# Hybrid attention and SSD block on one core: B and C split into rounded and low parts, their product as three rounded products

## Chip, core and metric

One core of a Trainium2 chip runs the whole kernel. The time is that of the device in microseconds, and lower is better. Four compute engines matter: TensorE (matmuls; its weight loads are listed apart as PEld), VectorE (DVE), ScalarE (ACT) and GpSimd (POOL), with SyncE (SP) issuing most of the DMAs. Each engine runs its own list of instructions in order and waits on semaphores for the others.

## What is computed

One layer of a block with 256 tokens, width 2048 and float32 data. Attention and a bidirectional Mamba-2 SSD stand side by side, then an MLP. The part that the change touches is the SSD: for each of 8 groups, B and C (128 states x 256 tokens, after convolution and SiLU) are multiplied, masked and weighted with decays.

```python
def ssd_chunked(x, dt, A, Bm, Cm):
    xc = (x.astype(jnp.float32) * dt[..., None]).reshape(b, nc, CHUNK, g, h, p)
    Bc = Bm.reshape(b, nc, CHUNK, g, n)
    Cc = Cm.reshape(b, nc, CHUNK, g, n)
    ...
    cb = jnp.einsum('bclgn,bcsgn->bgcls', Cc, Bc)
    y_diag = jnp.einsum('bgcls,bghcls,bcsghp->bclghp', cb, Lmat, xc)
```

The SSD's result y is gated, `y * silu(z)`, and normalised within each group, then multiplied together with the attention's by w_out; the MLP is `x + jnp.square(jax.nn.relu(hm)) @ w_down`, with hm the normalised x times w_up.

## The kernel before

The large products stream the weights. A unit is a block of 512 columns of a weight matrix with all 2048 rows; it comes in 8 chunks of 256 rows, and a chunk is one slot of the program. A chunk is loaded into one of 8 buffers raw (SyncE, which waits until TensorE has used the buffer's last chunk), ScalarE copies it rounded into w_hi (line 495), VectorE subtracts to get w_lo, which lies in raw's place (line 836), and TensorE multiplies it in three rounded products, low x high, high x low, high x high: 12 matmuls of 128x512. ScalarE and VectorE work on the chunk four slots ahead (LEAD = 4). All matmuls go through one helper line, 1256; the rest of an operation's name in the profile tells which it is.

The small work of the SSD and the attention is laid between the slots. A window has 24 slots, and two groups of the SSD are handled in it. For a group, slots are counted as k from its start; the next group starts 12 slots later (GROUP_SLOT). The order is written by hand and is this:
- k = 3 to 9 of the previous group: VectorE's convolution of the new group (conv, line 876); k = 10: ScalarE's tanh (conv_t, line 543); k = 11: VectorE's silu writes xbc, whose parts 0 and 1 are x, part 2 is B, part 3 is C (line 881).
- k = 0: TensorE's group_products, after the slot's chunk: four transposes of x into the PSUM bank M0 (line 1332), then, once M1 is free, the product of B and C into M1, two matmuls of 128x256 in full precision.
- k = 1: VectorE masks the product (mask_cb, lines 887 and 889) and scales x (line 850).
- k = 2 to 5: VectorE multiplies the decays (mix, line 859). ScalarE makes the decays of the next group in slots 6, 7, 8 and 12 (line 533 to 539), and waits there for y_done, the semaphore of the y products that use the same buffers mix.
- k = 5 and 7: TensorE's y products from mix. k = 8: VectorE's gate (lines 895, 900). k = 9: squares (ScalarE line 560, VectorE 964 to 968). k = 10: TensorE sums them over the partitions. k = 11: VectorE's mean_sq (line 905), ScalarE's Ln and Exp (lines 563, 565), each with a table load. k = 12: VectorE's group_norm, four operations that end with gate_t (lines 910 to 918). k = 13 and 14: the result rounded and its low part.

Slot k = 12 of one group is slot k = 0 of the next. In it VectorE does the w_lo of the slot, then group_norm; TensorE does its chunk, then group_products of the new group.

The groups 1 to 6 start in windows of the projection, and group 7 in the first window of attention, between 0 and 400 us of the program; group 0 starts in the first window, at slot 20, where no group is ahead of it.

Of the kernel before, what the change touches and what calls it, by code (L numbers as in the profile page):

```python
# [28 lines left out]
P = 128  # L29
SEQ, D_MODEL = 256, 2048  # L30
# [49 lines left out]
def build(nc, x, norm_mix_g, w_in, q_norm_g, k_norm_g, rel_bias, conv_w, conv_b, dt_bias, a_log,  # L80
# [18 lines left out]
    with ctx:  # L99
# [77 lines left out]
        rnorm = place("rnorm", [P, SEQ], at=at_of(lo2, 1024))  # L177
        newton = place("newton", [P, SEQ], at=at_of(lo2, 1024))

        sq_hi = place("sq_hi", [P, SEQ], f32r, at=cat_base + 32768)  # L180
        sq_lo = place("sq_lo", [P, SEQ], f32r, at=lo2[0] - 3072)
        gate_n = gate_t
# [65 lines left out]
        def sem(name):  # L248
            return ctx.enter_context(nc.semaphore(name))
# [36 lines left out]
        p_transposed, pT_ready, pv_done, att_hi, att_lo = (sem(n) for n in (  # L286
            "p_transposed", "pT_ready", "pv_done", "att_hi", "att_lo"))
        gate_summed = sem("gate_summed")
        first_tile_done, dt_half = sem("first_tile_done"), sem("dt_half")
        xres_in, added, squared_mid, mid_step = sem("xres_in"), sem("added"), sem("squared_mid"), sem("mid_step")  # L290
        rest_copied, hid_added, relu_squared, hid_hi_s, hid_lo_s, down_added, out_stored = (sem(n) for n in (
# [174 lines left out]
        def _(act):  # L466
# [74 lines left out]
            def conv_tanh_of(G):  # L541
                act.wait_ge(conv_step, 20 * (G + 1))
                act.activation(conv_t[:, :, :], conv[:, :, :], ACT.Tanh).then_inc(conv_tanh, 1)

            def next_group(G, i, k):

                if k in DECAY_SLOTS:
                    decays(G, DECAY_SLOTS[k])
                if k == 10:
                    conv_tanh_of(G)  # L550

            def ssd_slot(s, m, more=True):

                for i, o in enumerate(GROUP_SLOT):
                    G, k = 2 * m + i, s - o
                    if not 0 <= k < 16 or (i == 2 and not more):
                        continue
                    if k == 9:
                        act.wait_ge(gated, G + 2)
                        act.activation(gate_sq[:, :, :], gate[:, :, :], ACT.Square).then_inc(gate_squared, 1)  # L560
                    if k == 11:
                        act.wait_ge(m1_free, G + 2)
                        act.activation(log_ms[:, :], mean_sq[:, :], ACT.Ln).then_inc(ln_ready, 1)
                        act.wait_ge(ln_ready, G + 1)
                        act.activation(rnorm[:, :], log_ms[:, :], ACT.Exp, scale=-0.5).then_inc(rn_ready, 1)
                    if k == 13:
                        act.wait_ge(normed, G + 1)
                        for c in range(2):
                            ins = act.activation(cat_hi[:, ds(KT + 2 * G + c, 1), :], gate_n[:, c:c + 1, :], ACT.Copy,
                                                 scale=parB[:, ds(96 + 2 * G + c, 1)])  # L570
                        ins.then_inc(ssd_hi, 1)
                    if i != 1 or more:
                        next_group(G + 1, 1 - i % 2, k)
# [63 lines left out]
            for s in range(CH - LEAD, WIN):  # L637
                high_ahead(0, s)
                if s == 9:
                    act.wait_ge(rel_done, 1)  # L640
                    act.activation(relout[:, :], M1[0:HEADS, :], ACT.Copy).then_inc(rel_copied, 1)
                if s == 10:
                    act.wait_ge(rel_copied, 1)
                    act.dma_start(rel_rows, relout[:, :]).then_inc(rel_stored, 16)
                if s == 8:
                    act.wait_ge(dt_done, 1)
                    act.activation(dtv["r"][:, :], M0[64:128, 0:SEQ], ACT.Copy).then_inc(dt_half, 1)
                    act.wait_ge(x_rs, 1)
                    act.wait_ge(rs_spread, 1)
                    act.activation(rs_row[:, :], bank_pair(2)[:, 0, 0:SEQ], ACT.Copy).then_inc(rs_row_in, 1)  # L650
                if s == 9:
                    act.wait_ge(dt_step, 4)
                    act.activation(dtv["e"][:, :], dtv["e"][:, :], ACT.Exp, scale=-1.0).then_inc(dt_act, 1)
                    act.activation(dtv["soft"][:, :], dtv["v"][:, :], ACT.Relu).then_inc(dt_act, 1)
                if s == 13:
                    act.wait_ge(dt_step, 21)
                    act.dma_start(decay_rows[0:32, :].rearrange("h (c s) -> h c s", c=TT),
                                  prefix[0:32, :, 1:P + 1]).then_inc(decay_stored, 16)
                    act.dma_start(decay_rows[32:64, :].rearrange("h (c s) -> h c s", c=TT),
                                  prefix[32:64, :, 0:P]).then_inc(decay_stored, 16)  # L660
                    act.activation(dt_rows[0:32, 0:TT, :], prefix[0:32, :, 1:P + 1], ACT.Copy, scale=-1.0)
                    act.activation(dt_rows[32:64, 0:TT, :], prefix[32:64, :, 0:P], ACT.Copy, scale=-1.0)
                    act.activation(dt_rows[:, 3:5, :], dtv["soft"][:, :].rearrange("p (t s) -> p t s", t=TT), ACT.Copy)\
                        .then_inc(dt_act, 1)
                if s == 16:
                    act.wait_ge(decay_stored, 32)
                    src = decay_rows.rearrange("(d h) s -> d h s", d=2)[:, 0:PER_GROUP, :]
                    for d in range(2):
                        act.dma_start(decay[:, d], src[d:d + 1].broadcast_to([P, PER_GROUP, SEQ])).then_inc(decay_in, 16)
                if s in (8, 16):  # L670
                    stage_unit(0, s // CH - 1)
                if s == 10:
                    xbc_copy(0, 0, 0)
                    first_taps()
                if s == 18:
                    xbc_copy(1, 1, 0)
                if s == 17:
                    act.wait_ge(dt_tok, 1)
                    act.activation(tokn[:, :, :].rearrange("p a h -> p (a h)"), M1[:, 0:128], ACT.Copy, scale=-1.0)
                    act.activation(tokp[:, :, :].rearrange("p a h -> p (a h)"), M1[:, 0:320], ACT.Copy).then_inc(m1_free, 1)  # L680
                if s == 18:
                    conv_tanh_of(0)
                if s == 20:
                    act.wait_ge(m1_free, 1)
                if 20 <= s:
                    decays(0, s - 20)
                next_group(1, 1, s - GROUP_SLOT[2])
# [101 lines left out]
        def _(dve):  # L789
# [51 lines left out]
                low(U0 + n, j)  # L841


            def scale_x(G):

                dve.wait_ge(x_transposed, G + 1)
                for n, (xdt, H) in enumerate(((xdt_f, 4 * G), (xdt_b, 32 + 4 * G))):
                    dt = tokp[:, 3:5, ds(H, PER_GROUP)].rearrange("p t (h o) -> p t h o", o=1)\
                        .broadcast_to([P, TT, PER_GROUP, 64])
                    ins = tt_(xdt[:, :, :].rearrange("p t (h e) -> p t h e", e=64),  # L850
                              M0.rearrange("p (t h e) -> p t h e", t=TT, e=64), dt, ALU.mult)
                ins.then_inc(xtok_ready, 1)
# [95 lines left out]
            def ssd_slot(s, m, more=True):  # L948

                for i, o in enumerate(GROUP_SLOT):  # L950
                    G, k = 2 * m + i, s - o
                    if not 0 <= k < 16 or (i == 2 and not more):
                        continue
                    if k == 1:
                        mask_cb(G)
                        scale_x(G)
# [162 lines left out]
            for s in range(CH - LEAD, WIN):  # L1119
                if s > CH - LEAD:  # L1120
                    low_ahead(0, s)
                if s == 8:
                    dt_softplus(0)
                if s == 9:
                    parameters()
                if 10 <= s < 13:
                    dt_softplus(s - 9)
                if s == 12:
                    dt_sums()
                if s - GROUP_SLOT[1] != 3:  # L1130
                    next_group(0, 0, s - GROUP_SLOT[1])
                if s == 21:
                    dve.wait_ge(pool_masks, 4)
                    dve.wait_ge(m1_free, 1)
                    dve.wait_ge(params_ready, 6)
                    mask_cb(0)
                    scale_x(0)
                if s > 21:
                    mix_head(0, s - 22)
                next_group(1, 1, s - GROUP_SLOT[2])  # L1140
# [113 lines left out]
        def _(pe):  # L1254
# [71 lines left out]
            def group_products(G):  # L1326
# [6 lines left out]
                                           xbc[:, c, P * t:P * t + P], ident[:, :])  # L1333
                ins.then_inc(x_transposed, 1)
                pe.wait_ge(m1_free, G + 1)
                for t in range(TT):
                    ins = mm(M1[:, SEQ * (1 - t):SEQ * (2 - t)], xbc[:, 2, P * t:P * t + P], xbc[:, 3, :], True, True)
                ins.then_inc(cb_done, 1)

            def ssd_slot(s, m, more=True):  # L1340
# [252 lines left out]
```

## Time and profile before

| | |
|---|---|
| runs | 1519.38, 1519.98, 1521.73 us, median 1519.98 |
| profiled execution | 1518.61 us, its span 1516.9 us |
| TensorE busy | 1509.8 us, 100% of the span |
| VectorE busy | 962.8 us, 63% |
| ScalarE busy | 776.0 us, 51% |
| DMA | 291.42 MB, mean 192 GB/s |

The span is the time from the first to the last instruction in the profile; the execution's own time has 1.7 us around it. A row of a timeline gives the start, the duration, the engine, the line, the operation and what it writes and reads. Matmuls overlap: the start of one to the start of the next is what it takes of TensorE, not the duration in its row. A full-precision matmul leaves two records.

### The profile page before, as it was taken

To read this page: it belongs to the slowest core of one execution; us is meant where nothing else is said; L and a number is where in the kernel's file an instruction comes from. 1 tells how busy PE (TensorE), PEld (TensorE's weight loads), DVE (VectorE), ACT (ScalarE), POOL (GpSimd) and SP (SyncE) were. 2 spreads that over 40 slices of the span, in tenths; PEclk is the share of its full clock that TensorE was granted. 3 is DMA by queue.
4 is the path that set the end of the run, shared out by engine and by line. 5 is a ranking of instruction groups with operands and counts; after the bars stand their busy time and mean duration, and the time that the engine had idled before them with its cause. 6 is when DMAs were issued, how large, how long until landed. Compare 5 with 4: busy or idle time off the path is not lost.

```text
span 1516.9 us, 21034 instructions
## 1 busy us (share of the span) xinstructions
PE 1509.8 (100%) x7532; PEld 1265.7 (83%) x7532; DVE 962.8 (63%) x1265; ACT 776.0 (51%) x1103; POOL 25.7 (2%) x36
## 2 busy tenths in 40 slices
PE   8999999999999999999999999999999999999999
PEld 7888888888888888888888888888888888888887
DVE  6988989898766666665554665455545456545652
ACT  6687777776545455444444443334433434334531
POOL 1000000000000000000000000000000000000000
PEclk9999999999999999999999999999999999999999
DMA  9766667666665666666666656666666666666664
GB/s 251 230 194 188 188 193 189 189 212 210 205 183 172 182 174 181 209 203 192 185 190 181 191 185 193 194 192 185 193 194 194 187 188 194 194 191 186 192 194 139
DMA packets 188239, 291.42 MB, mean 192 GB/s; under 512 B 13645, under 2 KB 69327, under 8 KB 188160
## 3 DMA queue, kind: packets, MB, share of 16 engines
q1 hardware_dynamic: 185424, 285.99, 63.3%
q10 hardware_dynamic: 2736, 4.30, 0.9%
q8 instruction: 59, 0.97, 0.3%
q14 instruction: 20, 0.16, 0.0%
HBM read 288.05 MB, written 5.34 MB: 193 GB/s over the span
## 4 chain that ended last, share of the span: by engine, by line
PE 100%; DMA 0%; DVE 0%; issue 0%
PE psum L1256 97%; PE psum L1306 1%; PE psum L1322 1%; PE psum L1383 0%; PE psum L1403 0%; PE psum L1332 0%; DMA x_in<-in_x 0%; DVE acc L1231 0%; PE psum L1469 0%; PE psum L1428 0%; PE psum L1429 0%
## 5 line engine op out<-in xcount | busy, mean ns | idle before, releaser
L836 DVE TENSOR_TENSOR w_lo<-raw,w_hi 128x1024 fp32r<-128x1024 f32 x512 | 610.6, 1220 | 301.8 <-ACT w_hi L495 298.1
L495 ACT ACTIVATE w_hi<-raw 128x1024 fp32r<-128x1024 f32 x512 | 525.2, 1054 | 312.6 <-DMA raw<-in_w_down 154.5
L1256 PE MATMUL psum<-w_hi,actT 128*128 128x512 f32 x1536 | 497.7, 395 | 0.0
L1256 PEld LDWEIGHTS psum<-w_hi,actT 128*128 128x128 f32 x1536 | 288.4, 188 | 61.8 <-issue 3.0
L1256 PE MATMUL psum<-w_lo,actT 128*128 128x512 f32 x768 | 299.9, 390 | 0.0
L1256 PE MATMUL psum<-actT,w_hi 128*128 128x512 f32 x1024 | 256.4, 392 | 0.0
L1256 PEld LDWEIGHTS psum<-actT,w_hi 128*128 128x128 f32 x1024 | 184.4, 189 | 33.1
L1256 PE MATMUL psum<-w_hi,hid_lo 128*128 128x512 f32 x512 | 199.2, 389 | 0.0
L1256 PE MATMUL psum<-w_lo,hid_hi 128*128 128x512 f32 x512 | 199.2, 389 | 0.0
L1256 PE MATMUL psum<-w_hi,hid_hi 128*128 128x512 f32 x512 | 199.2, 389 | 0.0
L1256 PEld LDWEIGHTS psum<-w_lo,actT 128*128 128x128 f32 x768 | 144.4, 188 | 26.9
L1256 PEld LDWEIGHTS psum<-actT,w_lo 128*128 128x128 f32 x1024 | 139.7, 190 | 10.0
L1256 PE MATMUL psum<-actT,w_lo 128*128 128x256 f32 x1024 | 142.8, 282 | 0.0
L1256 PEld LDWEIGHTS psum<-w_hi,hid_hi 128*128 128x128 f32 x512 | 96.1, 188 | 20.0
L1256 PEld LDWEIGHTS psum<-w_hi,hid_lo 128*128 128x128 f32 x512 | 96.1, 188 | 19.9
L1256 PEld LDWEIGHTS psum<-w_lo,hid_hi 128*128 128x128 f32 x512 | 96.1, 188 | 19.8
L1256 PE MATMUL psum<-w_hi,cat_lo 128*128 128x512 f32 x256 | 100.8, 394 | 0.0
L1256 PE MATMUL psum<-w_hi,cat_hi 128*128 128x512 f32 x256 | 99.8, 390 | 0.0
L1256 PE MATMUL psum<-w_lo,cat_hi 128*128 128x512 f32 x256 | 99.8, 390 | 0.0
L1231 DVE SCALAR_TENSOR_TENSOR acc<-psum,inv_ms,acc 128x512 f32<-128x512 f32 x32 | 22.9, 747 | 117.0 <-PE psum L1256 117.0
L768 ACT ACTIVATE hid_sum<-psum 128x1024 f32<-128x1024 f32 x16 | 16.4, 1028 | 144.7 <-PE psum L1256 144.7
L1256 PEld LDWEIGHTS psum<-w_hi,cat_hi 128*128 128x128 f32 x256 | 48.1, 188 | 10.3
(197 smaller groups left out, 1033.8 us busy)
## 6 DMA issues: line engine op xcount, KB each, us to landing
raw<-in_w_in SPq DMA_DIRECT2D x128, 512.0 KB
raw<-in_w_up SPq DMA_DIRECT2D x128, 512.0 KB
raw<-in_w_down SPq DMA_DIRECT2D x128, 512.0 KB
raw<-in_w_out SPq DMA_DIRECT2D x64, 512.0 KB
raw<-in_w_in SPq DMA_DIRECT2D x64, 256.0 KB
raw<-in_w_in SPq DMA_DIRECT2D x128, 128.0 KB
decay<-decay_rows SPq DMA_DIRECT2D x14, 512.0 KB, 5.7
rel_tiles<-rel_rows ACTq DMA_DIRECT2D x4, 768.0 KB
```

The lines of the kernel that those rows point to most:

```text
L495: act.activation(w_hi[j][:, :, :], raw[j][:, :, :], ACT.Copy).then_inc(hi_ready, 1)
L768: act.activation(hid_sum[:, :, :], main_and_rest(n)[1], ACT.Copy).then_inc(rest_copied, 1)
L836: tt_(w_lo[j][:, :, :], raw[j][:, :, :], w_hi[j][:, :, :].bitcast(f32), ALU.subtract).then_inc(lo_dve, 1)
L1231: stt_(acc[:, n, t, :], bank_pair(n)[:, t, :], inv_ms[:, 2, t:t + 1], acc[:, n, t, :], ALU.mult, ALU.add).then_inc(down_added, 1)
L1256: return pe.matmul(o, lhsT, rhs, start=first, stop=last, **kw)
L1306: ins = pe.transpose(tiles(r)[:, c, P * t:P * t + P], stage[:, t, P * c:P * c + P], ident[:, :])
L1322: ins = pe.transpose(bank[:, SEQ * kk + P * t:SEQ * kk + P * t + P], src, ident[:, :])
```

## The change

ScalarE copies B and C of a group, rounded, into bc_hi. VectorE subtracts to get bc_lo. TensorE multiplies them as low x high, high x low and high x high, all rounded, in place of one full-precision product; there are two token tiles, so six matmuls of 128x256 in place of two. TensorE waits for bc_low in front of them, behind the transposes of x. ScalarE's copy stands at k = 0, behind the slot's w_hi and ahead of the other work of the slot; it waits for xbc and for the last group's product. VectorE's subtraction stands at k = 0 in the loop over the groups in flight.

```diff
+        bc_hi, bc_lo = (place(n, [P, 2, SEQ], f32r, at=cat_base + 12288 + 2048 * i) for i, n in enumerate(("bc_hi", "bc_lo")))
...
+            def split_bc(G):
+
+                act.wait_ge(xbc_ready, G + 1)
+                if positive(G):
+                    act.wait_ge(cb_done, G)
+                act.activation(bc_hi[:, :, :], xbc[:, 2:4, :], ACT.Copy).then_inc(bc_high, 1)
...
             def ssd_slot(s, m, more=True):
 
+                for i, o in enumerate(GROUP_SLOT):
+                    if s == o and (i != 2 or more):
+                        split_bc(2 * m + i)
...
                 if s == 20:
+                    split_bc(0)
                     act.wait_ge(m1_free, 1)
...
+            def low_bc(G):
+                dve.wait_ge(bc_high, G + 1)
+                tt_(bc_lo[:, :, :], xbc[:, 2:4, :], bc_hi[:, :, :].bitcast(f32), ALU.subtract).then_inc(bc_low, 1)
...
                     if not 0 <= k < 16 or (i == 2 and not more):
                         continue
+                    if k == 0:
+                        low_bc(G)
                     if k == 1:
                         mask_cb(G)
...
+                if s == 20:
+                    low_bc(0)
...
                 pe.wait_ge(m1_free, G + 1)
+                pe.wait_ge(bc_low, G + 1)
                 for t in range(TT):
-                    ins = mm(M1[:, SEQ * (1 - t):SEQ * (2 - t)], xbc[:, 2, P * t:P * t + P], xbc[:, 3, :], True, True)
+                    for n, (b, c) in enumerate(((bc_lo, bc_hi), (bc_hi, bc_lo), (bc_hi, bc_hi))):
+                        ins = mm(M1[:, SEQ * (1 - t):SEQ * (2 - t)], b[:, 0, P * t:P * t + P], c[:, 1, :], n == 0, n == 2)
                 ins.then_inc(cb_done, 1)
```

VectorE, slot 8 of a window, where one group is at k = 12 and the next at k = 0. Before:

```order
L836 TENSOR_TENSOR w_lo_67<-raw_59,w_hi_75 128x1024 [waits hi_ready]
L910 SCALAR_TENSOR_TENSOR newton<-rnorm 128x256 [waits rn_ready]
L911 ISA
L913 TENSOR_TENSOR newton<-newton,mean_sq 128x256 [waits m1_free,newton_step]
L914 REGISTER_ALU
L915 SCALAR_TENSOR_TENSOR rnorm<-newton,rnorm 128x256 [waits newton_step]
L916 REGISTER_ALU
L918 TENSOR_TENSOR gate_t<-gate,rnorm 128x512 [waits newton_step]
L835 REGISTER_ALU
L836 TENSOR_TENSOR w_lo_68<-raw_60,w_hi_76 128x1024 [waits hi_ready]
L887 TENSOR_TENSOR cbm<-psum,mask 128x2x256 [waits cb_done]
```

The same place after (lines are numbered by the new file):

```order
L849 TENSOR_TENSOR w_lo_67<-raw_59,w_hi_75 128x1024 [waits hi_ready]
L927 SCALAR_TENSOR_TENSOR newton<-rnorm 128x256 [waits rn_ready]
L928 ISA
L930 TENSOR_TENSOR newton<-newton,mean_sq 128x256 [waits m1_free,newton_step]
L931 REGISTER_ALU
L932 SCALAR_TENSOR_TENSOR rnorm<-newton,rnorm 128x256 [waits newton_step]
L933 REGISTER_ALU
L935 TENSOR_TENSOR gate_t<-gate,rnorm 128x512 [waits newton_step]
L859 TENSOR_TENSOR bc_lo<-xbc,bc_hi 128x512 [waits bc_high]
L848 REGISTER_ALU
L849 TENSOR_TENSOR w_lo_68<-raw_60,w_hi_76 128x1024 [waits hi_ready]
L904 TENSOR_TENSOR cbm<-psum,mask 128x2x256 [waits cb_done]
```

One operation is new, behind the last one of group_norm.

TensorE, the end of the chunk of a group's first slot and group_products. Before:

```order
L1256 MATMUL psum<-w_hi_75,actT 128x512
L1332 MATMUL psum<-ident,xbc 128x128 [waits m0_free,xbc_ready]
L1332 MATMUL psum<-ident,xbc 128x128 x3
L1256 MATMUL psum<-xbc 128x256 [waits m1_free]
L1256 MATMUL psum<-xbc 128x256
L1256 MATMUL psum<-w_hi_76,actT 128x512 [waits lo_dve]
```

After:

```order
L1277 MATMUL psum<-w_hi_75,actT 128x512
L1353 MATMUL psum<-ident,xbc 128x128 [waits m0_free,xbc_ready]
L1353 MATMUL psum<-ident,xbc 128x128 x3
L1277 MATMUL psum<-bc_hi,bc_lo 128x256 [waits bc_low,m1_free]
L1277 MATMUL psum<-bc_lo,bc_hi 128x256
L1277 MATMUL psum<-bc_hi 128x256
L1277 MATMUL psum<-bc_hi,bc_lo 128x256
L1277 MATMUL psum<-bc_lo,bc_hi 128x256
L1277 MATMUL psum<-bc_hi 128x256
L1277 MATMUL psum<-w_hi_76,actT 128x512 [waits lo_dve]
```

The two matmuls of xbc are six of bc_hi and bc_lo, and the first of them has the new wait; the next chunk's matmuls are behind it.

## Rows read from the trace of the kernel before

**Rows 1.** The page, the chain that ended last, by engine.

```profile
PE 100%; DMA 0%; DVE 0%; issue 0%
```

**Rows 2.** Waits of TensorE: us in total, times, longest us.

```profile
PE psum L1419 <- DMA rowsG<-in_norm_mix_g: 3.7, 1, 3.7
```

**Rows 3.** Timeline of TensorE, group 2: start, us, line, operation.

```profile
155.25 1.03 PE L1256 MATMUL psum<-xbc 128*128 128x256 f32 x4
155.93 0.58 PE L1256 MATMUL psum<-w_hi,actT 128*128 128x512 f32 x1
156.34 0.40 PE L1256 MATMUL psum<-w_lo,actT 128*128 128x512 f32 x1
```

**Rows 4.** Timeline of TensorE, the six rounded matmuls of attention scores.

```profile
435.27 0.28 PE L1256 MATMUL psum<-qkT_hi,qkT_lo 128*128 128x256 f32 x1
...
435.98 0.40 PE L1256 MATMUL psum<-w_hi,actT 128*128 128x512 f32 x1
436.22 0.40 PE L1256 MATMUL psum<-w_lo,actT 128*128 128x512 f32 x1
```

**Rows 5.** Timeline of ScalarE ahead of group 2's product.

```profile
144.50 0.62 ACT L560 ACTIVATE gate_sq<-gate 128x512 f32<-128x512 f32 x1
...
152.04 0.42 ACT L563 ACTIVATE log_ms<-mean_sq 128x256 f32<-128x256 f32 x1
...
154.10 1.04 ACT L495 ACTIVATE w_hi<-raw 128x1024 fp32r<-128x1024 f32 x1
```

**Rows 6.** Timeline of VectorE over the same stretch.

```profile
149.54 0.42 DVE L905 TENSOR_SCALAR mean_sq<-psum 128x256 f32<-128x256 f32 x1 [0.63 <-PE psum L1256]
...
151.91 1.22 DVE L881 SCALAR_TENSOR_TENSOR xbc<-conv_t,conv 128x1024 f32<-128x1024 f32 x1
155.18 1.23 DVE L836 TENSOR_TENSOR w_lo<-raw,w_hi 128x1024 fp32r<-128x1024 f32 x1 [2.05 <-ACT w_hi L495]
...
157.69 0.69 DVE L918 TENSOR_TENSOR gate_t<-gate,rnorm 128x512 f32<-128x512 f32 x1
```

**Rows 7.** Timelines of VectorE and TensorE, groups 1 and 7.

```profile
117.29 0.69 DVE L918 TENSOR_TENSOR gate_t<-gate,rnorm 128x512 f32<-128x512 f32 x1
...
115.87 1.03 PE L1256 MATMUL psum<-xbc 128*128 128x256 f32 x4
...
351.23 0.69 DVE L918 TENSOR_TENSOR gate_t<-gate,rnorm 128x512 f32<-128x512 f32 x1
351.94 1.23 DVE L836 TENSOR_TENSOR w_lo<-raw,w_hi 128x1024 fp32r<-128x1024 f32 x1
...
349.47 1.03 PE L1256 MATMUL psum<-xbc 128*128 128x256 f32 x4
```

**Rows 8.** Timelines at group 0, all engines.

```profile
73.64 1.26 ACT L533 ACTIVATE mix<-decay,tokn 128x128 f32<-128x128 f32 x4
...
73.97 1.22 DVE L881 SCALAR_TENSOR_TENSOR xbc<-conv_t,conv 128x1024 f32<-128x1024 f32 x1
...
75.10 1.22 DVE L836 TENSOR_TENSOR w_lo<-raw,w_hi 128x1024 fp32r<-128x1024 f32 x1
...
77.38 1.03 PE L1256 MATMUL psum<-xbc 128*128 128x256 f32 x4
```

**Rows 9.** Waits of ScalarE between 90 and 400 us.

```profile
ACT mix L533 <- PE psum L1256: 17.2, 14, 4.3
```

**Rows 10.** Timelines of VectorE and ScalarE, the w_lo of k = 9.

```profile
144.64 1.23 DVE L836 TENSOR_TENSOR w_lo<-raw,w_hi 128x1024 fp32r<-128x1024 f32 x1 [1.51 <-ACT w_hi L495]
...
181.80 1.05 ACT L495 ACTIVATE w_hi<-raw 128x1024 fp32r<-128x1024 f32 x1
...
183.36 1.22 DVE L836 TENSOR_TENSOR w_lo<-raw,w_hi 128x1024 fp32r<-128x1024 f32 x1
```

**Rows 11.** Timeline of TensorE at the start of the program.

```profile
5.01 3.20 PE L1256 MATMUL psum<-ident 128*128 128x128 f32 x14
8.00 0.73 PE L1322 MATMUL psum<-ident,x_in 128*128 128x128 f32 x4
```

More of the change, by code:

```diff
@@ L288, in build @@
         gate_summed = sem("gate_summed")
+        bc_high, bc_low = sem("bc_high"), sem("bc_low")
         first_tile_done, dt_half = sem("first_tile_done"), sem("dt_half")
```

## The prediction

> **What bounds the kernel now.** I read the page first: the chain that ended last is TensorE alone, 100% [rows 1]. The waits of TensorE come next: its only real idle time is the first DMA, 3.7 us [rows 2]; nothing later in the kernel has TensorE idle. So there is no slack anywhere behind the SSD part that could absorb a delay: every microsecond by which TensorE is held up, or made shorter, moves the end by a microsecond. The other engines matter only where TensorE waits for them, and today it never does. The change gives it something new to wait for. So the question is read from the timelines of TensorE, VectorE and ScalarE around the product of B and C, once in each of the eight groups (G = 0 to 7).
>
> **TensorE's own work.** Before, the product is two full-precision matmuls of 128x256, shown as four records. In group 2 they start at 155.25; the second 512-wide matmul behind them starts at 156.34 [rows 3]. One 512-wide matmul lies between, and takes 0.24 (435.98 to 436.22 [rows 4]). So the two products take 156.34 - 0.24 - 155.25 = 0.85 us. After, they are six rounded matmuls of 128x256. Exactly that shape and number stands in the attention scores: they start at 435.27, and the next work at 435.98, so 0.71 us [rows 4], 118 ns each. The gain is 0.14 us a group, 1.1 us in eight. Both are read to 0.01, so it lies between 1.0 and 1.3. Beside that row, the Trainium skill (TensorE: Matmul & The Clock Gate, Back-to-back issue gap) gives a gap of N/2.4 + 2.5 ns, an estimate of 109 ns for 256 columns; six would take 0.66, and the gain would be 1.7 us in all. The row's 118 ns decides.
>
> **The added work of the other two.** ScalarE gets one copy of 128x512 a group. A ScalarE operation of that size takes 0.62 [rows 5]. VectorE gets one subtraction of 128x512; its operation of that size from SBUF to SBUF takes 0.69 [rows 6]. Neither is long. What counts is where they stand. The copy stands behind w_hi of the group's first slot and needs xbc, which is there at 151.91 + 1.22 = 153.13 [rows 6], before that w_hi ends (154.10 + 1.04 = 155.14 [rows 5]). So bc_hi is ready at about 155.7 and holds nobody up. The work queued behind it on ScalarE (decays, stage, the next w_hi) is 0.5 us later, with four slots of lead over TensorE, so I put it at nothing.
>
> The subtraction is another matter. In VectorE's queue low_bc stands behind w_lo and behind the whole of group_norm of the previous group, four operations that end with gate_t at line 918. In group 2 that one starts at 157.69, and TensorE wants to start its product at 155.25 [rows 3, 6]. Today these have nothing to do with each other. After the change the product waits for bc_low, and so for the norm of another group.
>
> **The stall, group by group.** After the last gate_t starts, the next VectorE operation starts 0.71 later (351.23 to 351.94 in group 7 [rows 7]); the subtraction takes 0.69. The handover to TensorE I put at 0.15: between ScalarE and VectorE it is 0.04 (155.14 to 155.18 [rows 5, 6]), and about 0.1 for the weight load ahead of the first matmul is my estimate. So TensorE starts its product 1.55 us after gate_t starts. By group:
> - G1: gate_t at 117.29, product wanted at 115.87, 1.42 + 1.55 = 3.0 us [rows 7].
> - Even groups, G2: 157.69 - 155.25 = 2.44, so 4.0 us [rows 3, 6]. G4 and G6 show the same difference to 0.01.
> - Odd groups, G7: 351.23 - 349.47 = 1.76, so 3.3 us [rows 7]. G3 and G5 show the same.
> The even ones are longer because ScalarE there does a stage copy and a conv_in copy more in front.
> Sum: 3.0 + 3 x 4.0 + 3 x 3.3 = 24.9 us.
>
> G0 has no norm in front. xbc is ready at 75.19, the copy at 75.85; VectorE is in w_lo until 76.3, so bc_lo is done at about 76.95 and the product could start at 77.1, wanted at 77.38 [rows 8]. No stall, by a margin of 0.3 us. ScalarE however holds back its first decays from 73.64 until the copy is done, some 2.2 us; it has idle time ahead of group 1 and four slots of lead, so I cost this at nothing; without that cover it would be 2 us once.
>
> **Does the stall repeat?** One could think that the first stall gives VectorE and ScalarE a lead that shortens the next. That is so only where they are held by their own work. ScalarE's decays wait for TensorE's y products, 14 times in this stretch, two for each of seven groups [rows 9]. There it is tied to TensorE again, five slots ahead of the product, whatever lead it had. From there runs a chain without a gap: decays, w_hi, w_lo (which in the even groups waits 1.51 for that w_hi [rows 10]), the last conv taps, conv_tanh, w_hi, table load, Ln at 152.04, table load, Exp, w_hi at 154.10, w_lo at 155.18, the norm [rows 5, 6]. So in even groups the stall repeats in full. In the odd groups VectorE comes late to one link: w_hi is done at 181.80 + 1.05 = 182.85, w_lo starts at 183.36 [rows 10]. With a lead it would start 0.5 us earlier, and the chain with it. I take 0.5 off for G3, G5 and G7: 24.9 - 1.4 = 23.5 us.
>
> **Sum.** The profiled execution took 1518.6. 1518.6 + 23.5 - 1.1 = 1541.0. It lies 1.4 under the median of the runs, 1519.98; so against the median 1542.4. Its own range: the handover and the spacing may be off by 0.2 a group (1.4 us), the odd groups by 1.4, ScalarE's later work by 0.5 a group (3.5): 1538 to 1547.
>
> **Rivals.**
> 1. The stalls are as said, and TensorE's clock falls in them. The rows of the start show half rate (1.2 in place of 2.4 GHz): 14 full-precision records of 128 columns between 5.01 and 8.00 are 0.214 each [rows 11], as long as a record of 256 columns in group 2 (0.85 / 4). Before that TensorE had been idle for 3.7 us [rows 2], and stalls of 3 to 4 us are of that size. The slow stretch lasted at most from 3.7 to 8.0, 4.3 us, of which half, 2.1, was lost. If the three longest stalls bring it back: 1542.4 + 3 x 2.1 = 1549. If all seven: 1557. Against it: each stall stands alone in 39 us of full work. Beside it, the Trainium skill (TensorE: Matmul & The Clock Gate, Part 1) says that the array's clock falls to half after it has been idle and comes back only after sustained work, which is a rule against this change; whether gaps as short as these suffice, no row here shows.
> 2. The lead is kept after all: if ScalarE's Ln could start when mean_sq is there (149.54 + 0.42 [rows 6]) in place of 152.04 [rows 5], bc_low would come 2.1 us earlier in the even groups, and the stall would be about 1.9 in each of them; with the same 1.9 in the others, 13 us in all, 1519.98 + 13 - 1.1 = 1532. It decides for this if the ScalarE operations in front are done before the norm's sum; the tie to the y products speaks against it.
> 3. Not slower: bc_low comes in time. This needs the chain from the y products to bc_low to be 3 to 4 us shorter than the rows show, the point being bc_lo done before 115.7 in group 1, or that TensorE finds other work ahead of the waiting matmul, which its order does not have. Then only the gain is left: 1519.98 - 1.1 = 1518.9, within 0.2%.
> 4. The change doesn't do what it says: were the six matmuls handled at full precision, they would take 6 x 0.43 = 2.6 in place of 0.85, 14 us more in eight groups, 1558. The attention rows speak against it: same kind of operands, 0.12 each.
>
> **How the numbers follow.** Forecast 0.76, clock falls in some or all of the gaps 0.12, lead kept 0.08, not slower 0.03, full precision 0.01. The range holds the forecast's own 1538 to 1547, most of what lies between it and rival 2, and the clock's three-stall case: 1535 to 1550. A measurement of this kernel tells about 0.2% (3 us) from no change. Slower by more 0.96, within 0.2% 0.03, faster 0.01.
>
> **What would show each step.** In the profile after: TensorE has new waits for bc_lo, seven of 2.8 to 4.1 us, none in G0, 23 to 25 us in all, and its busy share falls to about 98%; the waits alternate long (even) and short (odd). bc_hi takes 0.62, bc_lo 0.69 and stands right behind gate_t. The six rounded matmuls take 0.71. The matmuls behind a stall are 0.23 apart if the clock holds, 0.43 if it falls. It would be wrong if the waits were missing, all near 2 us, or if VectorE idled ahead of bc_lo.

## The result and the profile after

| | before | after |
|---|---|---|
| runs | median 1519.98 us (1519.09 to 1521.73, 5 runs) | median 1549.94 us (1548.28 to 1555.9, 5 runs) |
| profiled execution | 1518.61 us | 1548.28 us |
| TensorE's mean granted clock | 1.000 | 0.996 in the profiled run; 0.994, 0.994, 0.996, 0.989 in the others |

The ratio is 1.0204, 95% interval 1.0193 to 1.0215: slower by 30 us. The prediction was 1542.4, 7.5 us less, with a range that ended at 1550; two of the five runs lie above that, and the ratio times the median before is 1551. The sign, the place and the size of the stalls came as forecast; that the clock would hold in them did not.

The page of the changed kernel, its first part and the chain that ended last, to be read beside [rows 1]:

```profile
PE 1517.4 (98%) x7548; PEld 1271.4 (82%) x7548; DVE 968.2 (63%) x1273; ACT 779.6 (50%) x1111; POOL 25.7 (2%) x36
...
PE 91%; ACT 3%; DVE 3%; issue 2%; DMA 0%; DVEq 0%; SPq 0%; ACTq 0%
```

The chain was TensorE alone; now it passes through ScalarE and VectorE. The waits of TensorE (us in total, times, longest) have one new row, beside that of [rows 2]:

```profile
PE psum L1277 <- DVE bc_lo L859: 21.9, 7, 3.7
```

Seven waits, none of them in group 0. TensorE around three of them, groups 1, 2 and 3 (start, us, operation, and in brackets the idle time before it and who ended it), beside [rows 3, 7]:

```profile
116.29 0.60 PE L1353 MATMUL psum<-ident,xbc 128*128 128x128 f32 x4
119.58 0.35 PE L1277 MATMUL psum<-bc_hi,bc_lo 128*128 128x256 f32 x1 [2.69 <-DVE bc_lo L859]
...
158.46 0.60 PE L1353 MATMUL psum<-ident,xbc 128*128 128x128 f32 x4
162.77 0.55 PE L1277 MATMUL psum<-bc_hi,bc_lo 128*128 128x256 f32 x1 [3.71 <-DVE bc_lo L859]
163.12 0.41 PE L1277 MATMUL psum<-bc_lo,bc_hi 128*128 128x256 f32 x1
163.33 0.42 PE L1277 MATMUL psum<-bc_hi 128*128 128x256 f32 x1
...
202.22 0.60 PE L1353 MATMUL psum<-ident,xbc 128*128 128x128 f32 x4
205.51 0.36 PE L1277 MATMUL psum<-bc_hi,bc_lo 128*128 128x256 f32 x1 [2.70 <-DVE bc_lo L859]
```

Before, the transposes of group 2 start here, and the product 0.44 us later, at 155.25 [rows 3]:

```profile
154.81 0.60 PE L1332 MATMUL psum<-ident,xbc 128*128 128x128 f32 x4
```

So the product is later by 119.58 - 116.29 - 0.44 = 2.85 us in group 1, 3.87 in group 2, 2.85 in group 3. Groups 4 to 7 read 3.86, 2.86, 3.87 and 2.81. Sum 23.0 us. The idle time in brackets adds up to less (21.9), because it begins where the last matmul ended, not where the next could have started.

Group 0 has no row among the waits, but it is not quite free of them either:

```profile
77.73 0.60 PE L1353 MATMUL psum<-ident,xbc 128*128 128x128 f32 x4
78.30 0.35 PE L1277 MATMUL psum<-bc_hi,bc_lo 128*128 128x256 f32 x1
```

bc_lo runs on VectorE from 77.47 to 78.15, and the product starts 0.15 later, 0.57 behind the transposes. Where bc_lo was early (group 0 of the kernel with bc_lo ahead of the norm, below) it starts 0.35 behind them. So group 0 is 0.2 us late here.

Who is late is in VectorE's timeline of group 2, beside [rows 6]:

```profile
158.82 1.22 DVE L849 TENSOR_TENSOR w_lo<-raw,w_hi 128x1024 fp32r<-128x1024 f32 x1 [2.05 <-ACT w_hi L497]
...
161.33 0.69 DVE L935 TENSOR_TENSOR gate_t<-gate,rnorm 128x512 f32<-128x512 f32 x1
161.94 0.68 DVE L859 TENSOR_TENSOR bc_lo<-xbc,bc_hi 128x512 fp32r<-128x512 f32 x1
162.56 1.23 DVE L849 TENSOR_TENSOR w_lo<-raw,w_hi 128x1024 fp32r<-128x1024 f32 x1
```

bc_lo ends at 162.62 and TensorE starts at 162.77. VectorE never waits for bc_hi: bc_lo starts as soon as gate_t lets it.

The other part of the loss is the clock. In group 2 the matmuls behind the stall are 0.21 us apart (163.12 to 163.33), in group 1 they are 0.12. The granted clock in stretches of 4 us behind the stalls of groups 2, 3, 4, 5, 6 and 7 (each row: the stretch, its length, the busy time of TensorE, its weight loads, VectorE, ScalarE and GpSimd, then the clock as a share of full speed, the DMA share and GB/s):

```profile
162.00:166.00 4.00, 3.23 (x11) 2.88 (x12) 3.36 (x7) 4.00 (x6) 0.00 (x0) 0.57 0.04 12
205.00:209.00 4.00, 3.49 (x14) 2.94 (x15) 2.92 (x5) 3.16 (x5) 0.00 (x0) 0.73 0.18 65
209.00:213.00 4.00, 4.00 (x20) 3.32 (x20) 3.59 (x6) 1.13 (x2) 0.00 (x0) 0.84 0.19 35
250.00:254.00 4.00, 3.71 (x14) 3.08 (x15) 4.00 (x7) 3.68 (x6) 0.00 (x0) 0.66 0.00 1
254.00:258.00 4.00, 4.00 (x18) 3.27 (x17) 4.00 (x6) 0.00 (x0) 0.00 (x0) 0.92 0.27 71
293.00:297.00 4.00, 3.80 (x21) 3.29 (x22) 2.92 (x6) 2.85 (x5) 0.00 (x0) 1.00 0.05 19
336.00:340.00 4.00, 3.61 (x12) 3.16 (x13) 3.53 (x6) 3.78 (x6) 0.00 (x0) 0.57 0.00 0
379.00:383.00 4.00, 3.81 (x20) 3.32 (x21) 4.00 (x7) 4.00 (x7) 0.00 (x0) 1.00 0.30 112
```

It fell in groups 2, 3, 4 and 6 and held in 1, 5 and 7, so the long stalls all had it and one of the four short ones. The clock time that was not granted is (1 - 0.57) x 4 = 1.72 us in group 2, 1.08 + 0.64 = 1.72 in group 3, 1.68 in group 4, 1.72 in group 6, 6.8 us in all. That is the most that the falls can have cost, because clock that is not granted while TensorE still waits costs nothing.

What they did cost shows in the distance from one group's transposes to the next group's. In groups 1 and 5, where the clock held, it is 2.79 and 2.80 us more than before. Their stalls are 2.85 and 2.86, so behind a stall the rounded product saves 0.06 us and not 0.14. In groups 2, 3, 4 and 6 the distance is 5.27, 4.39, 5.42 and 5.38 us more; less the stall, and with the 0.06, the falls took 1.46, 1.60, 1.62 and 1.57 us, together 6.25.

The account of the profiled execution: stalls 23.0, the lateness in group 0 0.2, the clock 6.25, the product cheaper by 7 x 0.06 + 0.15 = 0.6, and 0.8 by which this execution was already later at its first product's transposes (77.73 against 76.95 before; the same 0.8 is there at its first weight chunk, 9.30 against 8.51, ahead of all that was changed). 23.0 + 0.2 + 6.25 - 0.6 + 0.8 = 29.65; measured 1548.28 - 1518.61 = 29.67. The falls are read from the same distances, so the sum says only that nothing is missing ahead of group 1 and behind group 7.

### The profile page after: what moved, and what is told of

The parts are those of the page before. It is cut to its first block, busy times and chain, and to the rows that moved or that the text cites. A ratio compares the mean times of both kernels' runs of the same rounds, so it can differ in the third digit from the quotient of the medians.

```text
span 1546.6 us, 21097 instructions
## 1 busy us (share of the span) xinstructions
PE 1517.4 (98%) x7548; PEld 1271.4 (82%) x7548; DVE 968.2 (63%) x1273; ACT 779.6 (50%) x1111; POOL 25.7 (2%) x36
## 4 chain that ended last, share of the span: by engine, by line
PE 91%; ACT 3%; DVE 3%; issue 2%; DMA 0%; DVEq 0%; SPq 0%; ACTq 0%
PE psum L1277 89%; ACT w_hi L497 1%; DVE conv L893 1%; DVE w_lo L849 1%; ACT L575 1%; PE psum L1327 1%; PE psum L1343 0%; PE psum L1426 0%; PE psum L1406 0%; DMA x_in<-in_x 0%; DVE bc_lo L859 0%; ACT conv_t L545 0%; ACT mix L535 0%; ACT stage L510 0%; DVE gate_t L912 0%
```

## Experiments

The theory to test had three parts: the whole loss lies in TensorE's wait for bc_lo and in the clock that falls in it; bc_lo is late because of its place in VectorE's queue; and a stall gives the next odd group a lead. Each has a rival below.

**The added work without the wait.** TensorE keeps the old product.

```diff
                 pe.wait_ge(m1_free, G + 1)
-                pe.wait_ge(bc_low, G + 1)
                 for t in range(TT):
-                    for n, (b, c) in enumerate(((bc_lo, bc_hi), (bc_hi, bc_lo), (bc_hi, bc_hi))):
-                        ins = mm(M1[:, SEQ * (1 - t):SEQ * (2 - t)], b[:, 0, P * t:P * t + P], c[:, 1, :], n == 0, n == 2)
+                    ins = mm(M1[:, SEQ * (1 - t):SEQ * (2 - t)], xbc[:, 2, P * t:P * t + P], xbc[:, 3, :], True, True)
```

> ScalarE and VectorE make bc_hi and bc_lo as in the changed kernel, but TensorE takes the old full-precision product and waits for neither. Theory (everything that was lost lies in TensorE's wait and in the clock that falls in it): within 1 us of before, no wait of TensorE after the start, clock 1.000, ratio 1.000. Rival (the added work of the two engines itself costs time, by pushing their later work): some us above before, up to 6 for what the wait's 23 us do not explain, ratio up to 1.004.

Measured: 1520.02 us, ratio 1.0001 (0.9991 to 1.0011), clock 1.000, no wait of TensorE for bc_lo. The added work by itself is hidden, to within the 0.1% that this can tell. The trace shows one small thing that the time does not: the stage copy of ScalarE, 1.0 us later than before and half of it by bc_hi, is now just late for TensorE's transposes. The first rows are TensorE in the slot behind group 3's first slot, with the transposes of stage 0.36 behind the start of the chunk's last matmul. Before, they follow it by 0.23 (197.11 to 197.34), as the last row shows:

```profile
198.00 0.39 PE L1277 MATMUL psum<-w_hi,actT 128*128 128x512 f32 x1
198.36 1.09 PE L1327 MATMUL psum<-ident,stage 128*128 128x128 f32 x8
```

```profile
197.34 1.03 PE L1306 MATMUL psum<-ident,stage 128*128 128x128 f32 x8
```

So 0.1 us is lost there, and 0.7 in all from group 1 to group 7 (transposes at 115.99 and 350.30, 234.3 apart, against 233.6 before).

**The wait without the rounded product.**

```diff
                 pe.wait_ge(bc_low, G + 1)
                 for t in range(TT):
-                    for n, (b, c) in enumerate(((bc_lo, bc_hi), (bc_hi, bc_lo), (bc_hi, bc_hi))):
-                        ins = mm(M1[:, SEQ * (1 - t):SEQ * (2 - t)], b[:, 0, P * t:P * t + P], c[:, 1, :], n == 0, n == 2)
+                    ins = mm(M1[:, SEQ * (1 - t):SEQ * (2 - t)], xbc[:, 2, P * t:P * t + P], xbc[:, 3, :], True, True)
```

> The old full-precision product, but with the wait for bc_low ahead of it. Theory: seven waits as in the changed kernel, 23.0 us in all, the clock falls in some of them at about 1.7 us each, and the product is 0.14 us a group dearer than rounded: 1549 to 1557, about 1 us above the changed kernel for an equal number of falls. Rival (the clock falls because of the rounded products or of the switch between the two kinds of product): no falls, clock 1.000, 1520 + 23 = 1543.

Measured: 1552.71 us (1550.75 to 1553.87), ratio 1.0218 (1.0201 to 1.0235), clock 0.992 to 0.994. The waits are 21.9 us in seven, to the tenth those of the changed kernel. The clock falls in its profile behind groups 1, 2, 4, 5 and 6. Behind groups 1 and 5, whose waits are 2.70, the 512-wide matmuls are 0.42 and 0.43 apart, in place of 0.23:

```profile
121.44 0.63 PE L1277 MATMUL psum<-w_lo,actT 128*128 128x512 f32 x1
121.86 1.05 PE L1277 MATMUL psum<-w_hi,actT 128*128 128x512 f32 x2
...
295.96 0.63 PE L1277 MATMUL psum<-w_lo,actT 128*128 128x512 f32 x1
296.39 1.05 PE L1277 MATMUL psum<-w_hi,actT 128*128 128x512 f32 x2
```

So the clock falls without any rounded product, and the loss is the wait and the clock. It is 2.8 us above the changed kernel, where 1 was expected for an equal number of falls; its runs have a lower clock than most of that kernel's.

**The same waits with TensorE kept at work.** 24 matmuls on data that is there, into the bank that the product overwrites.

```diff
+                for _ in range(24 if G else 0):
+                    mm(M1[:, 0:SEQ], actT_hi[:, 0, 0:P], actT_hi[:, 0, :], True, True)
                 pe.wait_ge(bc_low, G + 1)
```

> The changed kernel, with 24 rounded matmuls of 128x256 on data that is there, into the bank that the product overwrites, ahead of the wait for bc_low in groups 1 to 7: they take 24 x 0.118 = 2.8 us, so that TensorE is idle for at most 1.1 us. Nothing is earlier or later than before but TensorE's activity. Theory: the end of each wait is set by VectorE and stays; the clock does not fall: clock 1.000, 1520 + 23.0 - 1.1 = 1542, ratio 1.0145, idle left 0.0 in odd groups and 1.1 in even ones. Rival (the 7 to 8 us above the waits come from elsewhere, so from work that the changed kernel adds): 1549 as the changed kernel.

Measured: 1541.42 us (1541.19 to 1542.03), ratio 1.0142 (1.0125 to 1.0159), clock 1.000 in every run. The stalls are where they were: TensorE's product starts 119.08 - 115.78 - 0.44 = 2.86 us late in group 1. What is left idle is 0.76 in the even groups:

```profile
115.78 0.60 PE L1353 MATMUL psum<-ident,xbc 128*128 128x128 f32 x4
119.08 0.30 PE L1277 MATMUL psum<-bc_hi,bc_lo 128*128 128x256 f32 x1
...
157.91 0.60 PE L1353 MATMUL psum<-ident,xbc 128*128 128x128 f32 x4
162.12 0.39 PE L1277 MATMUL psum<-bc_hi,bc_lo 128*128 128x256 f32 x1 [0.76 <-DVE bc_lo L859]
```

With nothing changed but that TensorE is busy while it waits, 8.5 us come back (1549.94 to 1541.42). That is the clock's share in the median run, and the rest, 22 us, is the stalls less the gain.

**Half of the filling.**

```diff
-                for _ in range(24 if G else 0):
+                for _ in range(12 if G else 0):
```

> As the filled one, but 12 matmuls of 1.4 us: TensorE is idle for 1.4 us in odd groups and for 2.4 us in even ones. Theory that the clock falls with some chance in an idle stretch of 2.7 to 3.7 us, and less often in a shorter one: 1542 to 1545, clock 0.998 to 1.000, falls if any in the even groups alone. Rival (any wait can make it fall): as many falls as the changed kernel, clock 0.994 to 0.996, 1549.

Measured: 1543.01 us (1542.73 to 1546.82), clock 0.999 in three runs and 0.996 in one. The profile has waits of 1.19 us in odd groups and 2.20 in even ones, and one fall, behind group 6's wait of 2.20. So idle time of 2.2 us can do it, and did once in three here. The run at 0.996 lost three to four falls' worth, which is every long wait at least; it was not profiled.

**Stalls in the odd groups alone.**

```diff
-                pe.wait_ge(bc_low, G + 1)
+                if G % 2:
+                    pe.wait_ge(bc_low, G + 1)
                 for t in range(TT):
+                    if G % 2 == 0:
+                        ins = mm(M1[:, SEQ * (1 - t):SEQ * (2 - t)], xbc[:, 2, P * t:P * t + P], xbc[:, 3, :], True, True)
+                        continue
                     for n, (b, c) in enumerate(((bc_lo, bc_hi), (bc_hi, bc_lo), (bc_hi, bc_hi))):
```

> Waits and rounded products in the odd groups alone (1, 3, 5, 7); the even ones take the old product with no wait, and all groups are split. Theory (a stall gives VectorE a lead that takes 0.5 us off the next odd group's chain, as the prediction had it, so without the long stall of the even group ahead there is no such lead): the waits of groups 3, 5 and 7 are 0.4 to 0.5 us longer than in the changed kernel, about 3.2 in place of 2.7, that of group 1 is 2.7 as there; sum of the four stalls, start to start, 12.8. Rival (the chain is tied to the y products for good and owes nothing to the stall before): 2.7 in all four.

Measured: 1541.48 us (two runs, 1540.54 and 1542.42), clock 0.994 and 0.993. The waits:

```profile
119.41 0.35 PE L1277 MATMUL psum<-bc_hi,bc_lo 128*128 128x256 f32 x1 [2.70 <-DVE bc_lo L859]
...
202.54 0.38 PE L1277 MATMUL psum<-bc_hi,bc_lo 128*128 128x256 f32 x1 [3.55 <-DVE bc_lo L859]
...
285.62 0.55 PE L1277 MATMUL psum<-bc_hi,bc_lo 128*128 128x256 f32 x1 [3.56 <-DVE bc_lo L859]
...
369.84 0.42 PE L1277 MATMUL psum<-bc_hi,bc_lo 128*128 128x256 f32 x1 [3.55 <-DVE bc_lo L859]
```

Group 1 waits as in the changed kernel; groups 3, 5 and 7 wait 0.85 longer than with a stall in the even group ahead (2.70). The lead is real, and larger than the 0.5 that I had expected. The missing 0.35 is not in the prediction's chain. The kernel with the split alone shows where it comes from: there gate_t of group 3 starts at 196.91 and the product at 194.62, 2.3 apart where it was 1.76 before, and groups 5 and 7 read the same, while the even groups keep their 2.44. So without stalls the odd groups' chain is 0.5 longer. That this is the added 0.6 us of VectorE and 0.5 of ScalarE a group is the likely reason; no run tests it. (Group 1 reads 2.4 in the kernel with the split alone and 1.4 in the changed one and in this one, though nothing ahead of it differs; that was not followed up.)

The clock (rows as above) fell behind all four stalls, also behind the 2.70 of group 1:

```profile
119.00:123.00 4.00, 3.59 (x14) 3.04 (x15) 2.92 (x5) 3.06 (x5) 0.00 (x0) 0.73 0.16 60
...
285.00:289.00 4.00, 3.38 (x11) 3.03 (x12) 2.92 (x5) 3.26 (x5) 0.00 (x0) 0.50 0.02 5
289.00:293.00 4.00, 4.00 (x18) 3.25 (x18) 3.69 (x6) 0.00 (x0) 0.00 (x0) 0.69 0.00 0
```

Behind group 5 it is at half for twice as long as behind any other stall: 2.00 + 1.24 = 3.2 us are not granted in these 8 us alone. By the distance of the transposes that fall took 2.7 us, those of groups 1 and 3 took 1.6. So four stalls lost 0.006 of the span by the clock, more than the seven of the changed kernel's profiled run (0.004) and as much as its middle runs.

**bc_lo ahead of the norm.**

```diff
             def ssd_slot(s, m, more=True):
 
+                for i, o in enumerate(GROUP_SLOT):
+                    if s == o and (i != 2 or more):
+                        low_bc(2 * m + i)
                 for i, o in enumerate(GROUP_SLOT):
...
-                    if k == 0:
-                        low_bc(G)
```

> low_bc stands ahead of group_norm (behind the slot's w_lo) in place of behind it. Theory (bc_lo is late because it stands in VectorE's queue behind the norm): bc_lo is ready 2.0 us earlier, so the waits are 0.7 us in odd groups and 1.7 in even ones, sum 23.0 - 7 x 2.0 = 9.0; idle that short does not let the clock fall: 1520 + 9 - 1.1 = 1528, ratio 1.005. Rival (bc_lo waits for something else, such as bc_hi): the waits stay above 2 us.

Measured: 1528.44 us (1527.59 to 1529.8), ratio 1.006 (1.0044 to 1.0075), clock 1.000. VectorE of group 2 and TensorE's wait:

```profile
156.29 1.23 DVE L849 TENSOR_TENSOR w_lo<-raw,w_hi 128x1024 fp32r<-128x1024 f32 x1 [2.05 <-ACT w_hi L497]
157.43 0.69 DVE L859 TENSOR_TENSOR bc_lo<-xbc,bc_hi 128x512 fp32r<-128x512 f32 x1
...
158.26 0.35 PE L1278 MATMUL psum<-bc_hi,bc_lo 128*128 128x256 f32 x1 [1.73 <-DVE bc_lo L859]
```

0.72 us in odd groups, 1.73 in even ones, 2.0 less each, as expected. Its place behind the norm was the cause of six tenths of the stalls (14 of 23 us) and of all the clock's loss. The rest, read from these rows and not tested, is the w_lo ahead of it, which waits 2.05 for ScalarE's w_hi behind Ln and Exp.

**The product one slot later.** In addition to bc_lo ahead of the norm, TensorE takes the product behind the next chunk, and VectorE masks it at k = 2.

```diff
                     if k == 0:
                         group_products(G)
+                    if k == 1:
+                        bc_product(G)
...
                     if k == 1:
-                        mask_cb(G)
                         scale_x(G)
+                    if k == 2:
+                        mask_cb(G)
```

> low_bc ahead of group_norm, and TensorE takes the product one slot later (k = 1, group 0 as it was), VectorE's mask at k = 2. Theory: one chunk of 2.7 us lies ahead of the product, more than the 0.7 and 1.7 us by which bc_lo would be late, so no wait is left, the clock stays at 1.000 and the gain of the rounded product shows alone: 1520 - 1.1 = 1518.9, ratio 0.9993. Rival (the mask, a slot later, delays mix and so the y products): new waits of TensorE for mix, above before.

Measured: 1521.58 us (1521.2 to 1522.88), ratio 1.0013 (1.0004 to 1.0023). The wait for bc_lo is gone, and I was wrong about the rest: a wait that I had not named has taken its place. TensorE's waits:

```profile
PE psum L1329 <- ACT stage L510: 2.2, 2, 1.1
```

and ScalarE in group 3's first slot:

```profile
194.49 0.62 ACT L552 ACTIVATE bc_hi<-xbc 128x512 fp32r<-128x512 f32 x1
195.01 1.27 ACT L535 ACTIVATE mix<-decay,tokn 128x128 f32<-128x128 f32 x4
...
197.29 1.23 ACT L510 ACTIVATE stage<-psum,small 128x512 f32<-128x512 f32 x2
```

The stage copy stands at the end of the slot, behind bc_hi and the decays, and the transposes of the next slot want it at about 197.3; they start at 198.58. Two things came together here. Counted from the transposes of x, the stage copy starts 1.3 us later than before (197.29 - 194.13 = 3.16 against 195.13 - 193.30 = 1.83), and TensorE wants it 0.8 us sooner (3.21 against 4.04), because the product no longer lies ahead of it. The first alone cost next to nothing: in the kernel with the split alone the copy is 1.0 later and TensorE lost 0.1.

**The stage copy ahead.**

```diff
-                    ssd_slot(s, m)
                     if s in (8, 16):
                         stage_unit(w, s // CH - 1)
+                    ssd_slot(s, m)
```

> The late product (e7), with ScalarE's stage copy of slots 8 and 16 moved ahead of the slot's SSD work, so that it no longer stands behind bc_hi. Theory (the 2.2 us above before in e7 are TensorE's waits for stage in the slot behind bc_hi): no wait for stage, bc_lo 1.1 us later in the odd groups but still ahead of the product, TensorE's stretch from group 1's to group 7's transposes 233.6 - 6 x 0.14 = 232.8 us against 235.8 in e7, time 1518.3, ratio 0.9993. Rival (the added operations of ScalarE and VectorE cost TensorE elsewhere too): the stretch stays above 233.6 and the time at or above before.

Measured: 1518.69 us (1518.4 to 1519.68, 11 runs) against 1519.46 of before (15 runs), ratio 0.9995 (0.9986 to 1.0004). No wait for bc_lo and none for stage; from group 1's transposes at 116.26 to group 7's at 349.26 it is 233.0 us, 0.6 less than before and 2.8 less than in the late product. The gain of the rounded product shows in the trace, 0.1 a group where 0.14 was expected (0.8 over these six). In the time it can't be told from no change.

## Why the prediction was right or wrong

- **What bounds the kernel**: right. Nothing behind the SSD part absorbed a delay; the 29.7 us are accounted for where they arise.
- **The product's gain**, 1.1 us: right in direction, too large in size. The six matmuls take 0.79 here (119.58 to 120.37), and also without a wait (77.76 to 78.55 in group 0 of the kernel with bc_lo ahead of the norm), and not the 0.71 of the attention scores: the first of them takes 0.20. Where nothing waits they start 0.35 behind the transposes in place of 0.44, and the gain is 0.15 after all; behind a stall it is 0.06. In the changed kernel that is 0.6 us. (The 1.7 us that stands beside the sum is 8 x (0.85 - 0.66) = 1.5; nothing hung on it.)
- **The stall, and that it is the norm of another group**: right, 23.0 us against 23.5. By group 2.85, 3.87 and 2.85 against 3.0, 4.0 and 2.8. In group 1 and the even groups 0.10 of the 0.13 to 0.15 too much is the step from gate_t to the next operation, 0.61 in place of 0.71. The margin of 0.3 us in group 0 was not there: it was 0.2 late. Moving bc_lo ahead of the norm took 2.0 us off each.
- **The stall repeats, and the odd groups get a lead**: right in what it says. That the odd groups came out at 2.8 is luck, from two errors that cancelled: the lead is worth 0.85, not 0.5, and the odd groups' chain is 0.5 longer in the new kernel, which the prediction cost at nothing.
- **ScalarE's copy at nothing**: right while the stalls cover it, nearly so without them (0.7 us), wrong once the product was also moved: then TensorE wanted the stage copy sooner, and it came 1.1 us late in two groups. "Four slots of lead" held for w_hi, but the stage copy has no such lead; it is wanted in the next slot.
- **The clock holds**: this is the step that failed. The sum went by the forecast without a fall, at 0.76, and gave the rival with falls 0.12. So the sum's term for the clock was nothing. The runs show in its place: the clock fell in every run of the changed kernel, 6.3 us in the profiled one, 8.5 in the median (1549.94 against 1541.42 with TensorE kept at work), and 14.5 in the slowest (1555.90 against 1541.42), whose mean clock is 0.989. The price was near, 1.5 to 1.6 us a fall where I had bounded 2.1. That the rival's three-stall case gave 1549 where 1549.94 came is in part luck: it had three falls at 2.1, and the profiled run had four at 1.6. What was wrong is the reason that I gave against it, that each stall stands alone in 39 us of full work. How busy TensorE is before the stall did not protect it: all nine waits of 3.5 to 3.7 us that were profiled have a fall behind them. The start of the program had shown idle time of 3.7 us ahead of half rate [rows 2, 11], and I noted that the stalls were of that size and gave it too little weight. The Trainium skill's rule (TensorE: Matmul & The Clock Gate, Part 1), that an idle array falls back to half rate, was the better guide than the row's surroundings; the 0.57 granted behind group 2's wait agrees with it.
- **The range** reached to 1550. The median lies 0.06 us inside it, by luck; the run at 1550.30 and the slowest, 6 us above, lie outside, and so does the ratio, 1551. The number of falls differs from run to run, and the range should have held all seven groups falling.

## What to carry to other kernels

Before a product is given a new operand from another engine, find the operation that makes it in that engine's queue and read when the one ahead of it ends; what stands ahead may belong to something else altogether. When an engine that is 100% busy gets a wait, add the clock to the wait: here 23 us of waiting cost 30. And in a slot that is full, look at every small operation behind the new one for the one that is wanted soonest.

## What the runs showed of the hardware

TensorE's clock fell to half after idle time of 2.2 to 3.7 us in the middle of a fully busy stretch, not every time. By the idle time that TensorE's rows show:

| kernel | waits, us | falls in the profiled run | mean granted clock of its runs |
|---|---|---|---|
| filled | 0.8 at most | none | 1.000 in 4 |
| product one slot later | 1.1 twice | none | 1.000 in 11 |
| bc_lo ahead of the norm | 0.7 and 1.7 | none of 7 | 1.000 in 4 |
| half filled | 1.2 and 2.2 | none of 4 and 1 of 3 | 0.999, 0.999, 0.999, 0.996 |
| changed kernel | 2.7 and 3.7 | 1 of 4 and 3 of 3 | 0.996, 0.994, 0.994, 0.996, 0.989 |
| wait without the rounded product | 2.7 and 3.7 | 2 of 4 and 3 of 3 | 0.994, 0.992, 0.992, 0.994 |
| odd groups alone | 2.7 once, 3.6 three times | 1 of 1 and 3 of 3 | 0.994, 0.993 |

So waits of 3.5 to 3.7 us had a fall 9 times in 9, waits of 2.7 us 4 times in 9, of 2.2 us once in 3, and shorter ones in no profiled run. These are the waits of single profiled runs, few in number; they give an order and not a rate.

A fall took 1.7 us of granted clock and 1.5 to 1.6 us of time, with one exception: behind group 5 of the odd-groups kernel it was twice as long and took 2.7 us of time. At 1.7 us of granted clock a fall, 0.989 is worth ten falls in seven stalls, so some of the slowest run's were probably of that long kind; it was not seen, since only one run of each kernel is profiled. The clock need not be down when TensorE comes back: in group 3 of the changed kernel TensorE was back at 205.51, and the stretch of 205 to 209 at 0.73 is half speed for its last 2.2 us, so the fall came 1.3 us later, in the middle of work. Between a 2.70 us wait that kept the clock and one that lost it the rows show no difference, so what decides there stays open.

At the start of the program the profile's clock reads 1.00 from 0 to 12 us (kernel before), where the spacing of the matmuls shows half rate [rows 11]. So a mean clock of 1.000 says nothing of the start.
